# Two modulation groups move from TensorE products to row sums on VectorE

## The reference, cut to what matters

```python
s_lat = jax.nn.silu(c)
s_ctx = jax.nn.silu(c_ctx)
...
shift, scale, gate = jnp.split((s_lat @ w_mod[l] + b_mod[l])[:, None, :], 3, axis=-1)
shift_c, scale_c, gate_c = jnp.split(s_ctx @ w_mod[l] + b_mod[l], 3, axis=-1)
hx = _rmsnorm(x, norm_g[l]) * (1.0 + scale) + shift
hc = _rmsnorm(ctx, norm_g[l]) * (1.0 + scale_c) + shift_c
...
    ctx = ctx + gate_c * y_c
x = x + gate * y
```

## Time and profile before

| | |
|---|---|
| median of 3 runs | 2533.12 us (2531.54 to 2534.6) |
| span of the profiled execution | 2533.5 us |
| TensorE matmul busy | 2507.1 us (99%) |
| VectorE busy | 1919.9 us (76%) |
| ScalarE busy | 1272.7 us (50%) |
| weights and other data moved | 570.24 MB, 225 GB/s |

### The profile page before, as it was taken

One profiled execution on the slowest core, in us unless ns is written; L12 is line 12 of the kernel. 1 busy time (PEld: TensorE's weight loads), 2 busy tenths in 40 slices (PEclk: granted clock), 3 DMA queues, 4 the chain that ended last, 5 costly groups with the idle time before them and its releaser, 6 DMA issues.

```text
span 2533.5 us, 30785 instructions
## 1 busy us (share of the span) xinstructions
PE 2507.1 (99%) x11974; PEld 2046.0 (81%) x11974; DVE 1919.9 (76%) x2501; ACT 1272.7 (50%) x1754; POOL 98.0 (4%) x143
## 2 busy tenths in 40 slices
PE   8999999999999999999999999999999999999998
PEld 7777777888888888888788888888888888888887
DVE  6775776787866777667988868898875885888866
ACT  6534534545544444455446554445565454445654
POOL 0000000000000000000200000020000000200000
PEclk9999999999999999999999999999999999999999
DMA  9789589665656766687665567854546876544454
GB/s 355 260 311 316 200 283 313 208 226 200 218 197 213 253 234 232 231 260 278 197 214 170 180 249 251 310 166 150 166 141 242 292 256 233 183 154 147 149 193 173
DMA packets 350609, 570.24 MB, mean 225 GB/s; under 512 B 18096, under 2 KB 202800, under 8 KB 346624
## 3 DMA queue, kind: packets, MB, share of 16 engines
q1 hardware_dynamic: 343216, 532.87, 61.6%
q0 software_dynamic: 6528, 34.65, 3.8%
q10 hardware_dynamic: 720, 0.75, 0.1%
HBM read 559.79 MB, written 8.41 MB: 224 GB/s over the span
## 4 chain that ended last, share of the span: by engine, by line
PE 91%; DMA 4%; DVE 3%; ACT 1%; issue 1%; POOL 0%; SPq 0%; DVEq 0%; ACTq 0%
PE acc L597 27%; PE acc L599 27%; PE acc L598 27%; PE aux L1256 2%; PE aux L1281 1%; DVE w_lo L585 1%; PE aux L1035 1%; DMA raw<-in_w_o 1%; PE aux L1404 1%; DMA raw<-in_w_mod 1%; DMA xr_s<-c_mid 1%; DMA xr_s<-x_mid 1%; PE aux L1266 1%; DVE cacc L2519 1%; ACT w_hi L577 1%
## 5 line engine op out<-in xcount | busy, mean ns | idle before, releaser
L585 DVE TENSOR_TENSOR w_lo<-raw,w_hi 128x1024 fp32r<-128x1024 f32 x808 | 991.3, 1230 | 449.2 <-ACT w_hi L577 447.6
L577 ACT ACTIVATE w_hi<-raw 128x1024 fp32r<-128x1024 f32 x808 | 847.1, 1059 | 859.9 <-PE acc L599 795.9
L597 PE MATMUL acc<-w_hi,h_hi 128*128 128x512 f32 x2240 | 891.1, 398 | 8.7 <-DVE w_lo L585 8.6
L599 PE MATMUL acc<-w_hi,h_lo 128*128 128x512 f32 x2240 | 873.9, 390 | 0.0
L598 PE MATMUL acc<-w_lo,h_hi 128*128 128x512 f32 x2240 | 873.0, 390 | 0.0
L597 PEld LDWEIGHTS acc<-w_hi,h_hi 128*128 128x128 f32 x2240 | 421.3, 188 | 110.3 <-issue 21.3
L599 PEld LDWEIGHTS acc<-w_hi,h_lo 128*128 128x128 f32 x2240 | 420.9, 188 | 89.8
L598 PEld LDWEIGHTS acc<-w_lo,h_hi 128*128 128x128 f32 x2240 | 421.6, 188 | 83.6
L597 PE MATMUL acc<-w_hi,u_hi 128*128 128x512 f32 x800 | 318.6, 398 | 1.8 <-DVE w_lo L585 1.8
L599 PE MATMUL acc<-w_hi,u_lo 128*128 128x512 f32 x800 | 312.1, 390 | 0.0
L598 PE MATMUL acc<-w_lo,u_hi 128*128 128x512 f32 x800 | 311.8, 390 | 0.0
(11 more groups left out here) (355 smaller groups left out, 1971.4 us busy)
## 6 DMA issues: line engine op xcount, KB each, us to landing
raw<-in_w_in SPq DMA_DIRECT2D x631, 512.0 KB, 4.7
raw<-in_w_mod SPq DMA_DIRECT2D x112, 512.0 KB, 6.0
raw<-in_w_out SPq DMA_DIRECT2D x96, 512.0 KB, 4.7
rows_in<-in_w_mod SPq DMA_DIRECT2D x80, 512.0 KB, 6.6
raw<-in_w_rnn_out SPq DMA_DIRECT2D x32, 512.0 KB, 4.8
raw<-in_w_o SPq DMA_DIRECT2D x32, 512.0 KB, 5.4
raw<-in_w_attn_out SPq DMA_DIRECT2D x16, 512.0 KB, 5.5
xr_s<-x_mid POOLq DMA_DIRECT2D x4, 1024.0 KB, 13.7
```

The lines of the kernel that those rows point to most:

```text
L577: act.activation(w_hi[:, n % NSPLIT], raw[:, slot, (n % 2) * SK:(n % 2) * SK + SK], ACT.Copy).then_inc(hi_ready, 1)
L585: dve.tensor_tensor(w_lo[:, n % NSPLIT], raw[:, slot, (n % 2) * SK:(n % 2) * SK + SK], w_hi[:, n % NSPLIT].bitcast(F32), ALU.subtract).the ...
L597: pe.matmul(acc[pair][m][:, :], a_hi[:, k0 + k, tok], w_hi[:, s, k], start=b, stop=False)
L599: last = pe.matmul(acc[pair][m][:, :], a_lo[:, k0 + k, tok], w_hi[:, s, k], start=False, stop=e)
```

## The change

The two parts are split into halves too, so all twelve halves run as row sums: (0,0), (0,1), (1,0) twice each in the iterations, then (0,2) twice and (1,1) in the four chunks; the last three halves stay where they were, under new numbers 9 to 11. `CALM` and its search are gone; every half has its granules written out, from none to two row instructions at a granule. `part_tile`, `mod_products` and the semaphore `mod_used` go. The two halves of the gate group need 2x4 instead of 4 additions of gate rows and 8 small DMAs each way instead of 4. In the chunks, the row instructions now stand right behind `lo`, ahead of the attention's and the chunk's side work (in the iterations they stood there already). The halves 0 to 2 use the own places, half 3 uses an own place for every second tile, and the halves 4 to 8 the ring. Several waits are renumbered.

```diff
-Half = namedtuple("Half", "layer part half values slots first")
+Half = namedtuple("Half", "layer part half values slots at")
...
+    Half(0, 1, 0, 2, (0, None) * 4, tiles_at((SG1, (
+        33, 34, 35, 36, 42, 43, 44, 45, 46, 46, 48, 49, 50, 50, 53, 53, 54, 55)), (2 * SG1, (
+        0, 0, 2, 4, 5, 5, 7, 7, 8, 10, 12, 12, 13, 13)))),
...
+    Half(0, 2, 0, 2, None, tiles_at((S2, (
+        17, 18, 18, 19, 20, 20, 21, 23, 24, 25, 26, 27, 29, 30, 31, 32, 34, 35, 36, 37, 38, 38, 39, 40, 41, 42, 43, 44, 45, 46, 48, 48)))),
+    Half(0, 2, 1, 2, None, tiles_at((S2, (
+        49, 50, 51, 52, 52, 53, 54, 55, 57, 58, 59, 60, 62, 63, 64, 65, 65, 66, 67, 68, 69, 70, 71, 72, 73, 73, 75, 76, 77, 78, 79, 80)))),
+    Half(1, 1, 0, 2, None, tiles_at((S2, (
+        81, 82, 83, 83, 85, 86, 88, 88, 90, 91, 92, 93, 94, 95, 96, 97, 97, 98, 99, 100, 102, 103, 104, 105, 106, 107, 107, 108, 109, 109, 110,
+        111)))),
...
-HOLD = 4
...
-PARTS = [(1, 0), (0, 2)]
-PART_AT = [26, 88]
...
+SUMS = [(h, TAIL_SG[0] + 15 if h == 9 else AT[h][-1] + 2) for h in range(len(HALVES))]
...
-            def mod_products(i, m):
-
-                if m == 0:
-                    pe.wait_ge(smod_r, 1)
-                    sums_free(SUMS.index(("part", i, PART_AT[i] + 6 * (KT // 2 - 1))))
-                tile = "part", i, m
-                pe.wait_ge(*landed(tile))
-                for j in range(NCH):
-                    last = pe.matmul(X[3][32 * j:32 * j + 2, :], smod[:, m, :], raw[:, slot_of(tile), j, :], start=m == 0, stop=m == KT - 1)
-                last.then_inc(mod_used, 1)
...
             def sides(n):
                 attention_end(IT1 - 1, n)
-                mod_sides(S2 + n)
+                mod_events(S2 + n)
...
             for place in range(NCH * BIG2 + BIG3):
                 lo(dve, Q2, place)
+                mod_rows_of(S2 + place)
                 sides(place)
```

More of the change, by code:

```diff
@@ L105 @@
 HALF_TILES = KT // 2
[L106 to L111, removed]
@@ L129 @@
-HOLD = 4
[L130 to L141, removed]
-PARTS = [(1, 0), (0, 2)]
-PART_AT = [26, 88]
-SUMS = [("part", 0, 68), ("half", 0, 77), ("part", 1, 130), ("half", 1, 136), ("half", 2, AT[2][-1] + 3)]
@@ L158 @@
+AT = [x.at for x in HALVES]
+assert all(len(x.at) == 2 * x.values * HALF_TILES and x.at == sorted(x.at) for x in HALVES)
+SUMS = [(h, TAIL_SG[0] + 15 if h == 9 else AT[h][-1] + 2) for h in range(len(HALVES))]
+IS_GATE = [x.part == 2 for x in HALVES]
 COLUMNS_BEFORE = [sum(not g for g in IS_GATE[:e]) for e in range(len(SUMS) + 1)]
@@ L160 @@
 GATE_EVENTS = [e for e in range(len(SUMS)) if IS_GATE[e]]
-HALVES_BEFORE = [sum(k == "half" for k, _, _ in SUMS[:e]) for e in range(len(SUMS) + 1)]
-LAYER_COLUMNS = [1 + max(COLUMNS_BEFORE[e] for e in range(len(SUMS)) if not IS_GATE[e] and group(e)[0] == l) for l in range(LAYERS)]
+LAYER_COLUMNS = [1 + max(COLUMNS_BEFORE[e] for e in range(len(SUMS)) if not IS_GATE[e] and HALVES[e].layer == l) for l in range(LAYERS)]
 OPS_BEFORE = [0]
@@ L174, in rows_after, with own_slot, own_queue @@
     return OPS_BEFORE[h] + 2 * HALVES[h].values * (t + 1)
+def own_slot(item):
+    return HALVES[item[1]].slots[item[2]] if item[0] == "half" and HALVES[item[1]].slots else None
+def own_queue(item):
+    return None if own_slot(item) is None else own_slot(item) % 2
 LOADS, taken = [], 0
 BEFORE_PAIR = [[] for _ in range(GRANULES // 2 + 1)]
-for i, first in enumerate(PART_AT):
-    for m in range(KT):
-        BEFORE_PAIR[(first + 6 * (m // 2)) // 2].append(("part", i, m))
+FIRST_CLEAR = {0: 12, 1: AT[0][-1], 2: AT[1][-5], 9: S4 + 9, 10: X0 - 2, 11: C1 - 8}
 for h, x in enumerate(HALVES):
@@ L185 @@
         start = first - 2
-        if x.slots:
-            clear = AT[h][2 * x.values * (max(t - 2, 6 * (h == 7 and t == 7), 5 * (h == 5 and t == 6)) + 1) - 1] if t >= 2 else {0: 12, 1: AT[0][-1], 5: S4 + 9, 6: X0 - 2, 7: C1 - 8}[h]
+        if own_slot(("half", h, t)) is not None:
+            clear = FIRST_CLEAR[h]
+            if t >= 2:
+                clear = AT[h][2 * x.values * (max(t - 2, 6 * (h == 11 and t == 7), 5 * (h == 9 and t == 6)) + 1) - 1]
             start = min(max(first - 6, clear + 6), first)
@@ L194 @@
         taken = i + 1
-RING = [item for item in LOADS if item[0] != "half" or not HALVES[item[1]].slots]
+RING = [item for item in LOADS if own_slot(item) is None]
 PLACE = {item: n for n, item in enumerate(RING)}
 OWN = [item for item in LOADS if item not in PLACE]
[L200 to L207, removed]
 def own_before(item):
@@ L605, in chunk_of @@
         def chunk_of(e):
-            return modchunk2 if SUMS[e][:2] == ("half", 5) else modchunk
+            return modchunk2 if e == 9 else modchunk
         Q1, Q2 = 0, S2
+        U_FREE = (0, 2, 3, 5)
         part_acc = lambda it, c: acc[(it + c) % 2]
@@ L733, in _, with gate_bias, gate_rows @@
             pool.memset(rx[:, :, 0:PAD], 0.0).then_inc(mod_zero, 1)
[L737 to L742, removed]
-                pool.wait_ge(mod_chunk, GATE_EVENTS[i] + 1)
[L744 to L748, removed]
+            def gate_bias(l, i, half, values):
+                for j in range(2):
+                    for v in range(values):
+                        r, col = 32 * (values * j + v), HALF * half + CH * j
+                        pool.dma_start(gaterows[i][r:r + 1, :], t["b_mod_2"][l:l + 1, 2 * D + col:2 * D + col + CH]).then_inc(tables_in, 16)
+            def gate_rows(l, i, half, values):
+                pool.wait_ge(mod_chunk, GATE_EVENTS[i] + 1)
+                for j in range(2):
+                    for v in range(values):
+                        r, col = 32 * (values * j + v), HALF * half + CH * j
+                        pool.dma_start(m_mid[l, v:v + 1, col:col + CH], gaterows[i][r:r + 1, :]).then_inc(gate_out, 16)
+            pool.wait_ge(roped, 4 * NG * IT1)
+            gate_bias(0, 0, 0, 2)
             pool.wait_ge(oT_lo, IT1)
             pool.dma_start(rope2[:, :, :, :], t["axial_table"]).then_inc(tables_in, 16)
+            gate_rows(0, 0, 0, 2)
+            pool.wait_ge(mod_sums, 7)
+            gate_bias(0, 1, 1, 2)
+            gate_rows(0, 1, 1, 2)
             def source(s, src, xr):
@@ L855, in _ @@
             pool.wait_ge(m_lo_r, 2 * NCH)
+            pool.wait_ge(mod_sums, 9)
             source(0, t["ctx_2"][0], xr_p3)
@@ L1059, in mod_visit @@
             def mod_visit(n):
[L1061 to L1065, removed]
-                    if kind == "half" and n == at_granule:
-                        mod_half(e, h)
+                for e, (h, at_granule) in enumerate(SUMS):
+                    if n == at_granule:
+                        mod_half(h)
                     if not IS_GATE[e] and n == at_granule + 5:
@@ L1658, in sides @@
                     if n == BIG2 * chunk + 27 + 6:
-                        if chunk in (1, NCH - 1):
-                            act.wait_ge(mod_sums, 4 if chunk == 1 else 5)
+                        if chunk:
+                            act.wait_ge(mod_sums, (0, 6, 8, 8)[chunk])
+                            if chunk == NCH - 1:
+                                act.wait_ge(gate_out, 16 * 8)
                         for j in range(2):
@@ L1810, in stream @@
                         if s == 3:
-                            act.wait_ge(mod_sums, 8)
+                            act.wait_ge(mod_sums, 12)
                         act.activation(stg2[:, 0], pair[1][0][:, :], ACT.Sigmoid)
```

179 lines of the change are left out of this document (91 added, 88 removed).

## The result

The changed kernel takes **2544.2 us** (median of 4 runs, 2541.3 to 2544.9) where the kernel before takes 2533.5 on the same chip: ratio 1.0043, 95% interval 1.0031 to 1.0055. It is slower, by 11 us; predicted were 2545. The profiled execution has a span of 2542.2 us, 8.7 more than that of before.

What follows compares the result with a forecast made beforehand. TensorE's queued work plus few stalls was taken as the bound: span 2533.5 - 34.0 + 38 (ring chain) + 3 (earlier hops) + 5 (attention) = 2545.5, against the median 2545 us; 8-in-10 range 2504 to 2561.

Steps and rivals of the forecast that it cites:

- The 34 us off TensorE: Iterations and granules behind 193: removing the parts' visits, less added sums and columns, gives 34.0 us without new stalls.
- the floor of 518.9: Three iterations after the change: each the third's 171.5 us, plus four sums and one column set, 518.9 in place of 554.4.
- The chain of 16 hops: Ring, release at granule 268 to `lo` of 332: late releases chain over 221 us, making 38 us of waiting for `lo`.
- the lead of 4.8: At the ring's chain: PE's lead of 6.1 us less the last row's 1.3, subtracted from the waiting.
- My 6.2: Ring's chain: mean us from issue to `hi` with SyncE's reaction, from four loads of before, charged for 16 hops.
- The Trainium skill's 4.4 us for a pair: Ring loads: the page's fit for a pair's 1 MB, making the chain some 29 us shorter and the time about 2516.
- Attention's 5 us in the iterations: PE's transposes at granule 15 wait for `og` behind crowded rows: 5 us taken, bounds 0 to 10.
- 3 us for the granules 223 to 268: Ring hops ahead of granule 268: 3 us taken beyond existing stalls, bounds 0 to 6.
- Nothing behind granule 368: From granule 368 on, nothing changes: 0 us.
- Rival A: Chunks' ring: items are there when wanted, so the loads hide: 2499 to 2505 us, chance 0.24.
- Rival B: Chunks' ring: landing 5.2 us a hop, side work partly hidden, near no change: 2524 to 2532 us, chance 0.17.
- Rival C: Iterations: VectorE is the bound, attention ends cost 5 to 7 us each: 2560 to 2566 us, chance 0.12.

Runs made afterwards that it cites:

- Two lists calmed: Changed kernel with halves 6 to 8 in row pairs, two iteration-1 rows moved behind rope, half 5's last tile behind `og`: 2500.7 us, 0.9877 of the kernel before.
- two by two: Changed kernel with the rows of halves 6 to 8 in pairs at the first two granules of each four: 2509.6 us, 0.9910 of the kernel before.
- odd starts: Changed kernel with one row at each granule from 241 to 336 for halves 6 to 8, tiles starting at odd granules: 2585.8 us, 1.0209.
- odd and even: Kernel before, its last chunk half given one row per granule from 301 (odd) or 300 (even): 2553.8 us (1.0078) and 2534.0 us (1.0002).
- even starts: Changed kernel with one row at each granule from 242 to 337 for halves 6 to 8, tiles starting at even granules: 2514.4 us, 0.9929.

## Why the prediction was right, point by point

*The 34 us off TensorE.* Right, to some 2 us. *Two lists calmed* shows 32.7 of it as time. By its windows the products of the three iterations take 172.9 + 174.3 + 172.9 = 520.2 us, 1.3 more than the floor of 518.9. What I had too small is a half's sum: 0.97 us is its eight products alone, but the first iteration, which has one sum more than the window of 171.5, takes 1.4 us more. Behind granule 193 the columns are three sets (656.69, 783.79 and 1082.04), and I had counted two.

*The chain of 16 hops.* Right in its length and its mechanism, with two terms off in opposite directions; that they nearly cancel is luck. In the chain that ended last it runs from the issue at 840.34 to PE's granule 332 at 1058.01, 217.7 us against 221 predicted, with 16 transfers. Less the 178.7 us of TensorE and the lead of 4.8 that gives 34 us; the chunks took 34.5 more than in *two by two* (269.7 and 235.2). The landings were sized too long: SyncE's part and the transfers are 5.9 + 83.0 us, with the pauses between them some 90 instead of 99.2, or 5.4 us for each hop but the last. My 6.2 was the mean of four loads of before; why those took longer stays open. What is not landing was sized too short, 128 us instead of 122. Visible in the chain are two `sig` steps of ScalarE between the `hi` of one pair, at 969.41 (1.25 us), and the last row of each tile at its full 1.28 us, not at its step of 1.19 (1.4 us in all); the rest I did not split up. Of the waits I had told over ten of 2 to 4 us; there are 17, seven of them of 2.2 to 2.8 us and none longer, as part of the loss is slower steps. VectorE is busy 211.8 of 269.7 us (predicted 214 of 272).

*The Trainium skill's 4.4 us for a pair* ("DMA: Bandwidth & Descriptors", § Anatomy of one DMA) and its 2516 us: 15 of the 16 transfers on this chain took 4.8 to 5.3 us, and the last 8.2, where it was the third item of 1 MB issued within 5 us (from 1043.50 on); another such third item, at 824.46, took 7.2. Release to `hi` is 5.4 us, 1.0 above the page's number and 0.8 below my rows. The gain that I worked out from that number did not come, and with the rest of the chain as measured (128 us) it would still leave 15 us of loss in the chunks where 34 came. The page gives its fit for one DMA that GpSimd issues, and here a pair is two, and SyncE issues them.

*Attention's 5 us in the iterations.* Near in size, wrong in place. The iterations are 7.8 us above the floor of 518.9; 1.3 of that is the floor itself, the two waits for `qk` are 4.7, and 1.6 is a stretch at the lower clock behind the second of them, in iteration 2 (its window has 174.5 us of products, and *two lists calmed* 172.9), which is paid here, since TensorE is the bound. Behind the first, at 335.11, the clock stayed up (174.5 and 174.3). I had looked for the wait at `og` alone, and no wait for `og` stands in these windows.

*3 us for the granules 223 to 268.* The size came, by another way, which is luck: from granule 193 to 256 PE does not wait for `lo` at all. The 4.9 us of this stretch are 1.4 of the added sum (193.46 us of products in *two lists calmed*, 192.03 before), 0.4 by which the wait for `og` is longer than before (2.9 and 2.5), and 3.1 of slower products (196.5 and not 193.5; the clock is 0.98, and behind the end of that wait at 752.61 it is at the lower level). Up to granule 268 there is one wait for `lo`, of 0.24 us. *Nothing behind granule 368*: 3.5 us less, all of it behind 1200 us (1333.5 before, 1330.0 after), 1.6 as less idle time of PE. I did not trace it further.

*The total.* The span is 3.3 us below the sum's 2545.5: 2.8 from the chunks, 3.5 from behind granule 340 and 0.2 from ahead of the first mark, less 2.8 in the iterations and 0.4 from granule 193 to 256. That the time came within 1 us of 2545 is so in part luck; what the runs show is the mechanism and its size to some 3 us.

*Rival A* (the ring hides it, 2499 to 2505) did not come: the chunks took 269.7 us and not 236. Its condition, items there when they are wanted, is what *two by two* sets up, with 235.2. *Rival B* had the landing right (5.2 told, 5.4 measured) but wanted the rest 5 us shorter, and it was 6 longer. *Rival C* (VectorE the bound in the iterations, 2560 to 2566): its marks of 178 us and more did not come.

The prices also give the shifted lists afterwards. In a cycle of four granules with gap 2, three granules lie on the chain: 5.4 + 1.1 + 3 x (1.14 + 1.19) + 3 x 0.35 for sides (14.4 over the 41 granules of the sum) = 14.5 us, 3.4 above TensorE's 11.2. Over the 23 gaps of 2, less the lead, that is 73 us; the odd starts are 76.2 slower than *two by two*, and take 14.7 us a cycle. For the seven in the kernel before it is 19, measured 19.8 between odd and even. With gap 3 two granules lie on the chain, 11.9 us, and 11 us are left over, where the even starts are 4.8 slower (241.2 us for 21 cycles, 11.5 each), so there the sum is too high. My expectation for the odd starts was this same sum with 10 us of side work for all hops; at 0.35 a granule it is 24. That side work is priced by the sum of the changed kernel and was not read from the trace of the odd starts, and some landings there took longer than on the changed kernel's chain (8.4 us at 824.42, 7.0 at 870.86), so how the 14.7 us divide stays open.

## What to carry to other kernels

Where a ring is filled in a fixed order, each buffer has a gap: the time from its last reader to the first use of what comes next. List the gaps in the bound engine's granules, and where one is shorter than landing plus the steps to the first use, follow the hops to see whether they chain: a single short gap is covered by the lead, a row of them is paid in full. Then let a consumer read a buffer in a burst and give it back, and not spread its reads evenly: here two reads at each of two granules in place of one at each of four is worth 76 us against odd starts and 5 against even ones, with the same instructions. And where such a chain paces the engine, its own work there is free, and so is its slower clock.

## What the runs showed of the hardware

TensorE's granted clock fell to the lower of its two levels (0.51, 1.2 GHz) behind some waits of 2 to 3 us and not behind others: behind the wait of 2.34 us that ended at 862.77 it did, behind the one of 2.30 at 848.03 the next 6 us are at 1.00, and the longer waits of 2.83 and 2.73 us that ended at 929.75 and 957.16 had no such stretch behind them either. So the length of the last wait alone does not tell it. Each of the two stretches in the chunks took some 1.6 us. On the changed kernel's chain a pair of 1 MB lands in 4.8 to 5.3 us; as the third of three issued within 5 us (350 GB/s over the stretch from 1046.97 to 1055.64) it took 8.2.
